# A hybrid decoder layer on one core: down-projection weights with two adjacent rows per partition

## What is computed

```python
def expert_block(args):
    xb, e = args
    gu = xb @ w_gate_up[e] + b_gate_up[e]          # 1024 -> 2048
    gate, up = gu[:, :MOE_FF], gu[:, MOE_FF:]
    gate = jnp.minimum(gate, SWIGLU_LIMIT)
    up = jnp.clip(up, -SWIGLU_LIMIT, SWIGLU_LIMIT)
    act = (up + 1.0) * (gate * jax.nn.sigmoid(SWIGLU_ALPHA * gate))
    return act @ w_down[e] + b_down[e]             # 1024 -> 1024
```

## Time and profile before

| | us |
|---|---|
| median of 3 runs | 1317.52 |
| lowest and highest run | 1310.74 and 1319.14 |
| span of the profiled execution, first to last instruction | 1315.0 |
| TensorE busy in it | 1194.6 (91%) |
| VectorE, ScalarE, GpSimd busy | 342.2, 174.0, 100.0 |
| HBM read in it | 462.67 MB (10^6 bytes), 353 GB/s over the span |
| mean granted TensorE clock | 0.983 of full speed |

### The profile page before, as it was taken

The page is one execution under the profiler, slowest core; times in us unless marked ns, Lnnn a source line. Parts: engine busy times, 40 slices in busy tenths (PEclk is TensorE's granted clock), DMA queues, the critical chain, the costliest instruction groups (busy, mean ns, idle before and its releaser), DMA issues.

```text
span 1315.0 us, 15745 instructions
## 1 busy us (share of the span) xinstructions
PE 1194.6 (91%) x6295; PEld 610.6 (46%) x6295; DVE 342.2 (26%) x637; ACT 174.0 (13%) x268; POOL 100.0 (8%) x46
## 2 busy tenths in 40 slices
PE   2896999999899999999999999999999989999996
PEld 1696979978733333333334333333323333333331
DVE  0594347122332112112112212211111211122112
ACT  1454534210200000000000000000000000000001
POOL 0473434200000000000000000000000000000000
PEclk9897999999999999999999999999999999999999
DMA  9952492288679998999999999999999999999995
GB/s 331 299 176 70 133 324 88 97 315 365 260 280 408 416 417 353 366 418 417 417 417 417 418 418 419 418 418 418 418 417 417 417 417 418 419 418 418 418 417 234
DMA packets 105333, 464.24 MB, mean 353 GB/s; under 512 B 10937, under 2 KB 33714, under 8 KB 69458
## 3 DMA queue, kind: packets, MB, share of 16 engines
q1 hardware_dynamic: 100930, 461.19, 87.7%
q10 hardware_dynamic: 4320, 2.43, 0.6%
q0 software_dynamic: 48, 0.13, 0.0%
HBM read 462.67 MB, written 1.05 MB: 353 GB/s over the span
## 4 chain that ended last, share of the span: by engine, by line
PE 59%; DMA 18%; SPq 11%; DVE 6%; ACT 2%; issue 2%; ACTq 1%; POOL 0%; DVEq 0%
PE ps L411 57%; DMA ring<-in_w_gate_up_dram 17%; SPq L337 7%; SPq L341 4%; DVE ring L1204 3%; PE ps L824 1%; ACT kept L1115 1%; DVE kept L1500 1%; DVE ring L1202 1%; ACTq L917 1%; DMA kept<-in_x_dram 1%; DMA ring<-in_w_in_dram 0%; PE ps L419 0%; PE ps L843 0%; ACT w_hi L938 0%
## 5 line engine op out<-in xcount | busy, mean ns | idle before, releaser
L411 PE MATMUL ps<-ring,kept 128*64 128x512 f32 (+2 forms) x3296 | 716.6, 595 | 57.7 <-ACT kept L1115 23.4
L411 PEld LDWEIGHTS ps<-ring,kept 128*64 128x64 f32 (+2 forms) x3296 | 230.7, 137 | 513.3 <-issue 421.7
L411 PE MATMUL ps<-kept 128*128 128x128 f32 (+5 forms) x996 | 202.6, 412 | 7.4 <-DVE kept L1477 1.6
L411 PEld LDWEIGHTS ps<-kept 128*128 128x128 f32 (+2 forms) x996 | 114.3, 179 | 89.3 <-issue 78.0
L1507 DVE TENSOR_SCALAR kept<-ps 128x512 f32<-128x512 f32 x32 | 22.1, 691 | 454.8 <-PE ps L411 454.8
L1111 ACT ACTIVATE kept<-kept 128x512 f32<-128x512 f32 x32 | 20.2, 630 | 788.7 <-DVE kept L1507 788.7
L1526 DVE TENSOR_TENSOR kept<-ps,kept 64x512 f32<-64x512 f32 x64 | 44.1, 689 | 272.5 <-PE ps L411 271.5
L1580 POOL TENSOR_TENSOR w_lo<-ring,w_hi 128x1024 fp32r<-128x1024 f32 x38 | 93.5, 2479 | 139.6 <-ACT w_hi L938 139.6
L411 PE MATMUL ps<-ring 128*128 128x128 f32 (+4 forms) x560 | 83.9, 307 | 1.3 <-issue 1.3
L411 PEld LDWEIGHTS ps<-ring 128*128 128x128 f32 (+3 forms) x560 | 76.4, 189 | 9.0 <-issue 5.1
L411 PE MATMUL ps<-hT_hi,w_hi 128*128 128x256 f32 x272 | 78.4, 288 | 0.6 <-POOL w_lo L1580 0.6
(11 more groups left out here) (218 smaller groups left out, 466.4 us busy)
## 6 DMA issues: line engine op xcount, KB each, us to landing
ring<-in_w_gate_up_dram SPq DMA_DIRECT2D x256, 1024.0 KB, 20.3
ring<-in_w_down_dram SPq DMA_DIRECT2D x128, 1024.0 KB, 22.2
ring<-in_w_ada_dram SPq DMA_DIRECT2D x24, 1024.0 KB, 5.5
ring<-in_w_in_dram SPq DMA_DIRECT2D x22, 1024.0 KB, 12.5
ring<-in_w_out_dram SPq DMA_DIRECT2D x4, 1024.0 KB, 14.5
ring<-in_w_o_fox_dram SPq DMA_DIRECT2D x2, 1024.0 KB, 8.7
ring<-in_w_o_delta_dram SPq DMA_DIRECT2D x2, 1024.0 KB, 11.1
kept<-in_x_dram SPq DMA_DIRECT2D x1, 1024.0 KB, 10.2
```

Source lines behind the costliest of these rows:

```text
L411: return pe.matmul(dst, lhsT, rhs, start=start, stop=stop, skip_group_check=True)
```

## The change

The two rows of a chunk that a partition receives are now adjacent in memory: partition p gets rows 2p and 2p + 1, one run of 8 KB. Each chunk's two contraction steps are then the even and the odd rows of its 256, so the transposes take every second column of `gate_a` within a block of 256, and `down` picks the slice of `act_t` that belongs to each step. The number of DMAs, their bytes, the number of transposes and matmuls and all waits stay.

```diff
             def load_dn(e, j):
-                sp.dma_start(ring[:, 16 + j, :].rearrange("p (k n) -> p k n", k=2),
-                             w_down[0, e, j * 256:(j + 1) * 256, :].rearrange("(k p) n -> p k n", p=P)).then_inc(
+                sp.dma_start(ring[:, 16 + j, :],
+                             w_down[0, e, j * 256:(j + 1) * 256, :].rearrange("(p k) n -> p (k n)", k=2)).then_inc(
                     expert_chunk_sem(16 + j), 16)
...
             def act_transposes(i, par):
                 pe.wait_ge(S("act_ready"), i * 2 + (par + 1))
+                pairs = gate_a.rearrange("s (j p k) -> s j k p", j=2, k=2)
                 for j in range(4):
-                    last = pe.transpose(bank(7, j * P, P), gate_a[:, j * P:(j + 1) * P], ident)
+                    last = pe.transpose(bank(7, j * P, P), pairs[:, j // 2, j % 2, :], ident)
                 last.then_inc(S("act_t_ps"), 1)
...
                     for kk in range(2):
                         k = 2 * j + kk
-                        lhsT = act_t[:, (k % 4) * P + (k // 4) * 64:(k % 4) * P + (k // 4) * 64 + 64]
+                        at = (2 * (j % 2) + kk) * P + (j // 2) * 64
+                        lhsT = act_t[:, at:at + 64]
                         for d in range(2):
```

## The result

The changed kernel takes 1306.91 us, the median of 20 runs (1300.56 to 1313.40); the kernel before takes 1317.31 us in 20 runs beside it (1306.56 to 1319.64). The ratio is 0.9937 with a 95% interval of 0.9921 to 0.9954, which is 8.3 us less, between 6.1 and 10.4 us. The profiled execution spans 1304.6 us where before it spanned 1315.0 us, so 10.4 us less. So the ratio says 8, the medians and the two profiles say 10; the forecast was 6.8. Where the rest comes from is a question for the experiments.

A forecast was written before the change was run, and what follows sets the result against it. The DMA stream of weights after its last idle time, near 532.7 us, was taken as the bound; 25 experts x 0.27 us = 6.8 us off 1317.5 us gave a median of 1310.7 us, range 1303 to 1317 us.

The forecast's parts named there:

- The bound: Expert loop: the weight stream, unbroken from about 532.7 us to the last gate/up landing at 1288.5 us, sets the end.
- The row's price: Down loads: each row costs a fixed 8.3 to 9.5 ns, so 8 KB rows raise 410 to 421 GB/s.
- The sum: Whole kernel: 0.27 us saved for each of experts 6 to 30, 6.8 us in all; other parts nothing.
- the restart: DMA engines start again near 532 us after their last idle time; its place was to hold within 0.5 us.
- the signs of being wrong: Restart over 2 us later, new idle time near 559 us, or gate/up windows moving as well.
- The pair's saving times the pairs: Stream behind the last idle time: 0.5 to 0.6 us less for each of 12.5 expert pairs, 6 to 7.5 us.
- The transposes: TensorE's activation transposes reading every second column: taken as costing nothing, at most 2.6 us before the stream restarts.
- The slower rival: Stepped transposes each take X longer, delaying the restart by 24X, outweighing the saving from X = 0.28 us; chance 0.03.
- The rival's second sum: Slower transposes make TensorE the bound with 128X - 61; at X = 0.56 us 10.7 us above now, 1328 us.
- All rows gain: Gate/up rows in the stream speed up too: 1306.8 us at 424 GB/s, 1301.6 us at 427; chance 0.15.
- The rate hardly rises: Down loads: 410 GB/s belongs partly to the tensor or its place; median 1314.1 to 1317.5 us; chance 0.08.
- Lead lost: Stream's spare at 559 us too small, gain up to 755 us lost as idle time: 4.9 us, 1312.6 us; chance 0.07.

The follow-up runs named there:

- the second: Profiles of the kernel before and the changed kernel, both with the early masks' load issued by GpSimd instead of ScalarE: medians 1311.90 and 1306.03 us.
- the rows alone: Kernel before with only the down loads changed to 8 KB rows, transposes and slices as they were: 1306.61 us, ratio 0.9968.
- the medians without the early wait: Early masks' load moved from ScalarE to GpSimd: 1311.90 us on the kernel before, 1306.03 us on the changed kernel.
- the changed kernel with the stepped write: Changed kernel, but VectorE writes the activation in the transposes' order, so transposes read contiguous columns: 1307.68 us, ratio 0.9970.

## Why the prediction was right, and where it was off

**The bound.** Right: the stream from the last idle time on sets the end, not the point at 755 us where the chain changes. TensorE led for 85 us longer than before and the gain of that stretch was kept.

**The row's price.** Right in kind and size. A pair was to take 59.7 us and takes 59.63 us; halving the row moved the rate to the 387 that the same line gives, doubling it to 428. The down rows went from 410 to 421 or 422 and the gate/up rows stayed.

**The sum.** 6.8 us were forecast. The stream shows 6.5 us in the first pair of profiles and 7.2 us in the second, 5.6 us for the rows alone against the kernel before, and the medians without the early wait 5.9 us. The measured ratio of 8.3 us holds 6.8 us in its interval. That the two profiles differ by 10.4 us comes, to 4.0 us, from what lies ahead of the stream, where the masks' issue took 5.75 us for 11.03 us. I call that chance because the rows alone came with an issue of 11.38 us and the changed kernel with the stepped write with one of 0.44 us. The forecast that the restart keeps its place to within 0.5 us failed by it: it came 4.05 us earlier, and the change itself moves it 0.4 us the other way. The 3.8 us by which the median of 1306.9 us lies under the forecast of 1310.7 us are in none of the streams, so they say nothing for the sum, and that the range held them is owed to the microseconds allowed for scatter. None of the signs of being wrong came: no later restart, no new idle time, no faster gate/up windows. Such chance probably spreads the runs as well, though an issue was seen only in the profiled ones: the runs of the changed kernel fall into a group at 1300 to 1307 us and one at 1310 to 1313 us, and with the masks' load on GpSimd there is one group, 1304 to 1309 us.

**The pair's saving times the pairs.** 12.5 pairs by 0.62 us would be 7.7 us where the last landing shows 6.5 us. One microsecond is missing in the last pair and a half: in the kernel with the rows alone the last two gate/up transfers of the chain end 61.1 us apart (1223.68 and 1284.73 us), though a pair takes 59.6 us. The rate isn't what failed, it reads 421 GB/s in that window, which makes 25.7 million bytes where a pair has 25.17. So some of what stands behind the last gate/up unit in the queue seems to have come in ahead of its end, more than a pair earlier. Why stays open.

**The transposes.** Taken at nothing, they cost 0.12 us for each pair, 0.4 us at the restart, well below my bound of 2.6 us. My reason was wrong: I took the pace of the transposes as a sign that reading has room, but the stepped operand is the stationary one, whose load grew by half. The Trainium skill (page "SBUF — State Buffer", section "Door 1: The DMA port swizzle") lets two accesses to a 16-byte line run at full speed. The stationary load with just that step took 207 for 140 ns, and with one float of each line 209 ns, so the measurement decides against it here. The slower rival had the right direction, but each load's 0.07 us is mostly hidden behind the matmuls: of its X, the time that a transpose costs the path, some 0.02 us are left (0.12 us for eight), against 0.28 us from which it decides. The rival's second sum was wrong: the transposes at 443.1 us are those of the third expert, so fourteen periods lead to the last but one, which stands at 1263.8 us in the trace, and not to the last at 1293 us. TensorE alone would thus have ended 32 us earlier, not 61 us, and at X = 0.56 us the rival's price would be some 40 us above the kernel before in place of 10.7 us. The forecast doesn't rest on it.

**The rivals.** All rows gain: no, gate/up rows beside 2 KB rows still run at 422. The rate hardly rises: no. The three cycles of the Trainium skill (page "DMA: Bandwidth & Descriptors", section "Why small descriptors are slow") would put 2 KB rows at 401 GB/s, an estimate from 410 and its 134 cycles in place of 131 for 4 KB. They run at 387. Lead lost: no idle time came back at 555 us.

## What to carry to other kernels

Where a stream of weights is the bound, count its rows, not only its bytes: here each row cost 9 ns on its engine, 6% of the time of a 4 KB row and 1.4% of a 16 KB one, and adjacent rows of the contraction can share a partition if the other operand's features are put in the same order, at a cost here of 0.12 us for each pair of experts while TensorE leads and nothing once the stream does. Find the last idle time of the DMA engines before you price a faster transfer: what arrives earlier ahead of it is worth nothing, everything behind it counts, also where TensorE still leads (12.5 pairs by 0.62 us gave 6.5 us of 7.7 us here). And compare stages before you believe a difference of spans: where one early DMA issue took 0.44 us in place of 11 us, the stream began 10 us sooner, more than the change is worth.

## What the hardware showed beyond that

The issue of one DMA of 896 KB held ScalarE for 0.44, 5.75 or 10.9 to 11.4 us in kernels whose code up to there is the same, while SP's loads were under way; with GpSimd issuing it, ScalarE went on at once and the runs drew together. What makes the issue long in one execution and short in another wasn't tried.

With half as many rows for the same bytes of down weights, the time from issue to landing of a gate/up load rose, from a median of 20.3 to 26.1 us, and with twice as many (rows of 2 KB) it fell to 17.3 us:

```profile
ring<-in_w_gate_up_dram SPq DMA_DIRECT2D x256, 1024.0 KB, 26.1
```

The issues of down loads late in the stream went by in bursts of 5.5 to 6 us, near TensorE's pace, where they had stretched to 12 us. That looks as if the queue's room were counted in rows rather than bytes, which I have only argued.

A VectorE multiplication of 128 by 512 floats went from 692 to 1068 ns when its result was written in alternation to two places 512 bytes apart.
